# A two-block transformer layer on one core: the router and the expert rows taken from the weighted residual, with 1/rms applied at the exit, the shift added on GpSimd, and the biases split beside the output product

## The reference

```python
def rmsnorm(x, w):
    xf = x.astype(jnp.float32)
    var = jnp.mean(xf * xf, axis=-1, keepdims=True)
    return (xf * lax.rsqrt(var + EPS) * w.astype(jnp.float32)).astype(x.dtype)

def modulate(h, shift, scale):
    return h * (1.0 + scale) + shift

h = h + g1 * (mix_x.astype(h.dtype) @ w_out[l])
h = h + g2 * moe(modulate(rmsnorm(h, norm_mlp_w[l]), sh2, sc2), w_router[l], b_router[l], ...)

# in moe: top 4 of 32 experts, tokens sorted by expert into blocks of 128
logits = (xt @ w_router + b_router).astype(jnp.float32)
top_vals, top_idx = lax.top_k(logits, TOP_K)
weights = jax.nn.softmax(top_vals, axis=-1)
...
dest = start_pad[sorted_e] + (jnp.arange(n_assign) - start_unpad[sorted_e])
...
gu = xblk @ w_gu[e] + b_gu[e]
gate, up = jnp.split(gu, 2, axis=-1)
act = (up + 1.0) * gate * jax.nn.sigmoid(SWIGLU_ALPHA * gate)     # both clipped before
return act @ w_down[e] + b_down[e]
```

## Time and profile before

| quantity | value |
|---|---|
| median of 3 runs | 3365.12 us (3364.69 to 3377.49) |
| profiled execution | 3372.43 us, span 3370.6 us |
| TensorE busy | 3107.6 us, 92% of the span |
| VectorE, ScalarE, GpSimd busy | 65%, 50%, 6% |
| conversion of a unit, ScalarE L456 (ring) | 795 times, 1054 ns |
| conversion of a unit, VectorE L464 (ring) | 795 times, 1217 ns |

### The profile page before, as it was taken

One profiled execution on the slowest core, in us unless ns is written; L12 is line 12 of the kernel. 1 busy time (PEld: TensorE's weight loads), 2 busy tenths in 40 slices (PEclk: granted clock), 3 DMA queues, 4 the chain that ended last, 5 costly groups with the idle time before them and its releaser, 6 DMA issues.

```text
span 3370.6 us, 37642 instructions
## 1 busy us (share of the span) xinstructions
PE 3107.6 (92%) x14074; PEld 2450.5 (73%) x14074; DVE 2177.8 (65%) x2497; ACT 1677.6 (50%) x1935; POOL 188.6 (6%) x179
## 2 busy tenths in 40 slices
PE   6989857999999999999978978999998998999998
PEld 2865556777777777777766756888887766788887
DVE  4555436999999999999976444443456557544345
ACT  2332334878877877777764212332234246432234
POOL 1054200000000000000002000000000000000000
PEclk9998967999999999999987978999999999999999
DMA  6246527999999999999955202323232210223220
GB/s 207 68 135 219 192 94 274 373 371 374 372 377 367 372 375 370 374 373 373 363 206 195 94 25 88 90 91 103 91 107 75 81 45 1 69 88 106 88 69 26
DMA packets 229490, 654.15 MB, mean 194 GB/s; under 512 B 21592, under 2 KB 40294, under 8 KB 228438
## 3 DMA queue, kind: packets, MB, share of 16 engines
q1 hardware_dynamic: 207408, 575.61, 47.7%
q0 software_dynamic: 10992, 45.73, 3.6%
q10 hardware_dynamic: 10902, 30.35, 2.4%
HBM read 614.39 MB, written 37.22 MB: 193 GB/s over the span
## 4 chain that ended last, share of the span: by engine, by line
PE 81%; DVE 12%; ACT 4%; issue 2%; DMA 1%; POOL 0%; DVEq 0%; ACTq 0%; SPq 0%; POOLq 0%
PE ps L272 78%; PE ps L284 3%; DVE arena L203 2%; ACT arena L237 2%; DVE arena L192 2%; ACT wunits L456 2%; DVE arena L199 2%; DVE ring_r L464 1%; DVE arena L211 1%; DVE H L192 1%; DMA arena<-in_ctx 1%; DVE arena L197 0%; DVE arena L215 0%; DVE arena_r L203 0%; DVE arena_r L464 0%
## 5 line engine op out<-in xcount | busy, mean ns | idle before, releaser
L464 DVE TENSOR_TENSOR ring_r<-ring,wunits 128x1024 fp32r<-128x1024 f32 x795 | 943.4, 1217 | 674.2 <-ACT wunits L456 658.3
L456 ACT ACTIVATE wunits<-ring 128x1024 fp32r<-128x1024 f32 x795 | 830.6, 1054 | 814.6 <-PE ps L272 793.5
L272 PE MATMUL ps<-arena_r,wunits 128*128 128x512 f32 (+1 forms) x3552 | 1112.3, 395 | 19.5 <-DVE arena_r L192 13.9
L272 PE MATMUL ps<-wunits,arena_r 128*128 128x512 f32 x3520 | 991.7, 399 | 3.2 <-DVE arena_r L192 3.2
L272 PEld LDWEIGHTS ps<-arena_r,wunits 128*128 128x128 f32 x3552 | 672.4, 190 | 168.9 <-issue 23.9
L272 PEld LDWEIGHTS ps<-wunits,arena_r 128*128 128x128 f32 x3520 | 658.7, 189 | 148.6 <-DVE arena_r L192 5.0
L272 PE MATMUL ps<-arena_r,ring_r 128*128 128x512 f32 (+1 forms) x1776 | 695.3, 391 | 0.0
L272 PE MATMUL ps<-ring_r,arena_r 128*128 128x512 f32 x1280 | 410.3, 391 | 0.0
L272 PEld LDWEIGHTS ps<-arena_r,ring_r 128*128 128x128 f32 x1776 | 337.8, 190 | 70.3
L272 PE MATMUL ps<-arena 128*128 128x128 f32 (+11 forms) x1368 | 236.6, 354 | 87.3 <-DVE arena L215 19.8
L464 DVE TENSOR_TENSOR arena_r<-arena,wunits 128x1024 fp32r<-128x1024 f32 x240 | 283.6, 1220 | 17.7 <-ACT wunits L456 11.4
(11 more groups left out here) (147 smaller groups left out, 1874.0 us busy)
## 6 DMA issues: line engine op xcount, KB each, us to landing
ring<-in_w_gu SPq DMA_DIRECT2D x382, 512.0 KB, 6.9
ring<-in_w_down SPq DMA_DIRECT2D x170, 512.0 KB, 5.5
arena<-in_w_gu SPq DMA_DIRECT2D x146, 512.0 KB, 6.8
arena<-in_w_down SPq DMA_DIRECT2D x94, 512.0 KB, 5.7
ring<-in_w_ada SPq DMA_DIRECT2D x48, 512.0 KB, 4.6
ring<-in_ffn_w_gate SPq DMA_DIRECT2D x44, 512.0 KB, 3.5
ring<-in_ffn_w_up SPq DMA_DIRECT2D x44, 512.0 KB, 3.6
ring<-in_ffn_w_down SPq DMA_DIRECT2D x40, 512.0 KB, 3.6
```

Of the source, the lines that this page charges most:

```text
L272: ins = self.e.matmul(o, l_, r_, start=start, stop=stop, skip_group_check=True)
L456: q.inc(q.e.activation(h, raw, ACT.Copy), (st.tag, "hi", i))
L464: q.inc(q.e.tensor_tensor(lo, raw, h.bitcast(F32), ALU.subtract), (st.tag, "lo", i))
```

## The change

The norm of the second half is not applied before the router any more. `HM` is now the residual times the gain, made tile by tile by ScalarE right behind the residual (`tile_act`), and TensorE adds a tile's share to the logits beside its squares (`tile_pe`). 1/rms multiplies the logits on VectorE and the token rows on ScalarE, when they leave PSUM. What the shift adds is worked out once: `shift_pe` turns its columns into a row by products with the identity, multiplies them with the router weights, and spreads both over the partitions with a product of ones. GpSimd adds the row to the token rows and stores them (`rows_pool`). The router, bias and table loads stand at the head of the stage, `pair` stays on in it, so that the shift and the biases advance beside the tiles. The routing has its prefix counts from two products and five additions, compares eight assignments in one operation, and leaves the expert weights to the end. The eight `MORE` slots are filled once the first gather has landed.

```diff
     def fetch(s, st, i):
...
-            if w.before[0] == "all":
+            if w.before[0] == "gathered":
+                barrier_of(s, "moe")
+                s.wait_ge(s_g[0], 16)
+            elif w.before[0] == "all":
...
-    MORE = [[s_more[i], lo, 0, ("all", "moe")] for i, lo in enumerate(
+    MORE = [[s_more[i], lo, 0, ("gathered",)] for i, lo in enumerate(
...
+    def tile_act(q, k):
+
+        q.wait_ge(*dve("resid", "mlp", k))
         if k >= q.squares:
-            q.wait_ge(*pe("ssq", tag, k - q.squares))
-        q.act(sqt(q, k), hk(k), ACT.Square, ("sq", tag, k))
-        yield
-        yield
+            q.wait_ge(*pe("ssq", "mlp", k - q.squares))
+        q.act(sqt(q, k), hk(k), ACT.Square, ("sq", "mlp", k))
+        q.act(HM[:, k, :], hk(k), ACT.Copy, ("hm", k), scale=gm2[:, k:k + 1])
+        yield
...
+    def tile_pe(p, k):
...
         for m in range(4):
             p.mm(PB[b][:, 2 * m:2 * m + 2], sqt(p, k)[:, m * 128:(m + 1) * 128], ones[:, 0:2], k == 0 and m == 0, k == 7,
...
+        p.wait_ge(*act("hm", k))
+        for t in range(4):
+            p.mm(PB[bl][:, t * 32:(t + 1) * 32], HM[:, k, t * 128:(t + 1) * 128], wr[:, k, :], k == 0 and t == 0, k == 7,
+                 "logits" if k == 7 and t == 3 else None)
+        yield
...
+    def shift_pe(p):
...
+        for k in range(8):
+            p.mm(PB[bs[k // 4]][0:1, (k % 4) * 128:(k % 4 + 1) * 128], M(3, k), ident, k % 4 == 0, k % 4 == 3,
+                 ("shift", k // 4) if k % 4 == 3 else None)
+        for k in range(8):
+            p.mm(PB[bs[2]][0:1, 0:32], M(3, k), wr[:, k, :], k == 0, False)
+        p.mm(PB[bs[2]][0:1, 0:32], ones[0:1, 0:1], br, False, True, ("shift", 2))
+        yield
+        yield
+        p.wait_ge(*dve("shift rows"))
+        for c in range(3):
+            b = p.bank(("shifts", c))
+            p.claim(("shifts", c))
+            x = srow[c] if c < 2 else brow
+            p.mm(PB[b][:, 0:x.shape[1]], ones[0:1, :], x, True, True, ("shifts", c))
...
     def out_act(q):
         q.limit = None
-        for i in range(U_IN, U_IN + NUNIT):
-            conv_hi(q, W, i)
-        q.slow.append(biases_act(q))
-        split_act(q, "mix", mixp, lambda k: MX[:, k, :])
-        q.wait_ge(*dve("parts", "mix", 7))
         load(q, "router", wr, I["w_router"][0].rearrange("(j p) n -> p j n", p=128))
         load(q, "router", br, I["b_router"])
+        biases_load(q)
         tab(q, "tri", 19456)
...
+        for i in range(U_IN, U_IN + NUNIT):
+            conv_hi(q, W, i)
+        q.slow += [shift_act(q), biases_act(q)]
+        split_act(q, "mix", mixp, lambda k: MX[:, k, :])
+        dense(q, conv_hi, W, [512, 512], 8, lambda c, m: q.jobs.append(tile_act(q, c * 4 + m)))
...
     def router_act(q):
-        roots_act(q, "mlp")
-        for k in range(8):
-            q.wait_ge(*dve("hm", k))
-            q.act(HM[:, k, :], HM[:, k, :], ACT.Identity, "hm", bias=M(3, k))
...
-                q.copy(xs[t % 2][:, h * 512:(h + 1) * 512], bank_of(("hmt", t, h))[:, :])
+                q.act(xs[t % 2][:, h * 512:(h + 1) * 512], bank_of(("hmt", t, h))[:, :], ACT.Copy, ("row", t, h),
+                      scale=rt[:, 2 * t:2 * t + 1])
                 q.free(("hmt", t, h))
-            q.own()
-            q.e.dma_start(hm_d[t * 128:(t + 1) * 128, :], xs[t % 2]).then_inc(s_hm[t % 2], 16)
...
+    def rows_pool(g):
         for t in range(4):
             for h in range(2):
+                x = xs[t % 2][:, h * 512:(h + 1) * 512]
+                g.wait_ge(*act("row", t, h))
+                g.tt(x, x, SROW[:, h * 512:(h + 1) * 512], ALU.add)
+            g.own()
+            g.e.dma_start(hm_d[t * 128:(t + 1) * 128, :], xs[t % 2]).then_inc(s_hm[t % 2], 16)
...
     def route_dve(v):
...
+        v.tt(LG, bank_of("logits")[:, 0:128].rearrange("p (t e) -> p t e", e=32),
+             rt.rearrange("p (t x) -> p t x", x=2)[:, :, 0:1].to_broadcast([128, 4, 32]), ALU.mult)
+        v.tt(LG, LG, BROW.unsqueeze(1).to_broadcast([128, 4, 32]), ALU.add)
...
+        for h in range(2):
+            is_ = slice(8 * h, 8 * h + 8)
+            v.tt(LH[:, is_, :], iota.unsqueeze(1).to_broadcast([128, 8, 128]),
+                 OF4[:, is_].unsqueeze(2).to_broadcast([128, 8, 128]), ALU.is_equal)
+            v.tt(RP[:, is_, :], iota[:, 0:48].unsqueeze(1).to_broadcast([128, 8, 48]),
+                 BK4[:, is_].unsqueeze(2).to_broadcast([128, 8, 48]), ALU.is_equal)
+            for t in (2 * h, 2 * h + 1):
+                v.ts(RH[:, 4 * t:4 * t + 4, :], RP[:, 4 * t:4 * t + 4, :], tokc[:, t:t + 1], None, ALU.mult, None,
+                     ("slots", t))
...
-        for i in range(16):
-            if i >= 2:
-                v.wait_ge(*pe("slots", i - 2))
-            v.ts(LH[i % 2], iota, OF4[:, i:i + 1], None, ALU.is_equal, None)
-            v.ts(RH[i % 2], iota[:, 0:NBLK], BK4[:, i:i + 1], tokc[:, i // 4:i // 4 + 1], ALU.is_equal, ALU.mult,
-                 ("slots", i))
...
+        v.wait_ge(*act("weights"))
+        v.reduce(SS, W4, ALU.add)
+        v.recip(SS, SS)
+        v.tt(W4, W4, SS.unsqueeze(2).to_broadcast([128, 4, 4]), ALU.mult)
...
     def moe_pool(g):
+        g.wait_ge(*dve("idx"))
+        g.wait_ge(*pe("hmt", 3, 1))
...
         gla_pe(p)
+        out_pe(p)
         p.pair = False
-        out_pe(p)
...
-        all_wait(p, "moe")
+        p.note(("all", "moe"))
```

More of the change, by code:

```diff
@@ new lines, in tile_act @@
+    def tile_act(q, k):
+        q.wait_ge(*dve("resid", "mlp", k))
+        if k >= q.squares:
+            q.wait_ge(*pe("ssq", "mlp", k - q.squares))
[3 more added lines that the diff above has]
+    def tile_pe(p, k):
+        if k == 0:
+            p.inuse.append(p.bank("ssq"))
+            p.inuse.append(p.bank("logits"))
+            yield
+        b, bl = p.banks["ssq"], p.banks["logits"]
+        p.wait_ge(*act("sq", "mlp", k))
+        if k == 0:
+            p.claim("ssq")
+            p.claim("logits")
+        for m in range(4):
+            p.mm(PB[b][:, 2 * m:2 * m + 2], sqt(p, k)[:, m * 128:(m + 1) * 128], ones[:, 0:2], k == 0 and m == 0, k == 7,
+                 ("ssq", "mlp", k) if m == 3 else None)
+        p.wait_ge(*act("hm", k))
[3 more added lines that the diff above has]
+        yield
@@ new lines, in tile_dve @@
+    def tile_dve(v, k):
+        yield
+    def shift_pe(p):
+        bs = [p.bank(("shift", c)) for c in range(3)]
+        p.wait_ge(*loaded("router"))
+        p.wait_ge(*dve("gm2"))
+        for c in range(3):
+            p.claim(("shift", c))
+        for k in range(8):
[4 more added lines that the diff above has]
+        p.mm(PB[bs[2]][0:1, 0:32], ones[0:1, 0:1], br, False, True, ("shift", 2))
@@ L1708, in roots_act, with shift_act @@
-    def roots_act(q, tag):
-        q.finish_jobs()
-        q.wait_ge(*dve("var", tag))
-        q.act(rt, rt, ACT.Sqrt, ("rt", tag))
-    def roots_dve(v, tag):
-        v.finish_jobs()
-        v.wait_ge(*pe("ssq", tag, 7))
-        v.ts(rt, bank_of(("ssq", tag))[:, 0:8], 1.0 / 1024, EPS, ALU.mult, ALU.add, ("var", tag))
-        v.free(("ssq", tag))
-        v.wait_ge(*act("rt", tag))
-        v.recip(rt, rt)
-        for m in range(4):
-            v.ts(dg[:, m, :], ident, rt[:, 2 * m:2 * m + 1], None, ALU.mult, None, ("dg", tag, m))
-        v.wait_ge(*pe("rms", tag))
+    def shift_act(q):
+        yield
+        yield
+        yield
+        for c in range(2):
+            q.wait_ge(*pe("shifts", c))
+            q.copy(SROW[:, c * 512:(c + 1) * 512], bank_of(("shifts", c))[:, :], ("shifts", c))
+            q.free(("shifts", c))
+        yield
@@ new lines, in shift_dve @@
+    def shift_dve(v):
+        yield
+        for c in range(2):
+            v.wait_ge(*pe("shift", c))
+            v.copy(srow[c], bank_of(("shift", c))[0:1, :])
+            v.free(("shift", c))
+        v.wait_ge(*pe("shift", 2))
+        v.copy(brow, bank_of(("shift", 2))[0:1, 0:32], "shift rows")
+        v.free(("shift", 2))
+        yield
+        yield
+        v.wait_ge(*pe("shifts", 2))
+        v.copy(BROW, bank_of(("shifts", 2))[:, 0:32])
+        v.free(("shifts", 2))
+        yield
@@ L1948, in route_dve @@
         v.reduce(SEL, OH.rearrange("p (t k e) -> p t e k", k=4, e=32), ALU.add, "sel")
+        v.fill(PF[:, 0, :], 0.0)
         v.wait_ge(*pe("ranks"))
-        v.copy(RKf, bank_of("ranks")[:, 0:128])
-        v.copy(CNT, bank_of("ranks")[:, 128:160])
+        sums = bank_of("ranks")[:, 128:256].rearrange("p (t e) -> p t e", e=32)
+        for t in range(4):
+            v.tt(PF[:, t + 1, :] if t < 3 else CNT, PF[:, t, :], sums[:, t, :], ALU.add)
+        v.tt(RKf, bank_of("ranks")[:, 0:128], a(o + 2700, 128), ALU.add)
         v.free("ranks")
@@ L1973, in route_dve @@
         v.stt(DF, BK4, 128.0, OF4, ALU.mult, ALU.add)
-        v.copy(DEST, DF)
+        for h in range(2):
+            is_ = slice(8 * h, 8 * h + 8)
[6 more added lines that the diff above has]
+                     ("slots", t))
+        v.wait_ge(*pe("slots"))
```

(12 more changed lines are left out.)

154 lines of the change are left out of this document (56 added, 98 removed).

## The result

| | before | after |
|---|---|---|
| first runs: median (lowest to highest) | 3365.12 us (3360.95 to 3377.49, 5 runs) | 3347.63 us (3344.90 to 3348.56, 5 runs) |
| ratio, 95% interval | | 0.9935 [0.9912, 0.9959] |
| timed again, on one chip | 3364.46 us (13 runs) | 3340.46 us (3333.22 to 3350.54, 6 runs), ratio 0.9932 [0.9912, 0.9953] |
| profiled execution | 3372.43 us, span 3370.6, clock 0.945 | 3345.97 us, span 3344.1, clock 0.948 |
| barrier to the gathered block's first transposes | 375.19 to 530.69: 155.5 | 372.77 to 500.31: 127.5 |

The account below looks back on a forecast made before the run. Experts bound by TensorE, so an earlier first gather counts fully: +6.5 and +8.7, tail -10.9, -14.8, -15.1, gather -4.6 give 30.2 us less, from 3365.1 to 3335 us. Range 3320 to 3350.

Parts of the forecast that it names:

- one to one: Experts: bound by TensorE, so time won ahead of them should reach the kernel's end in full.
- Steps 1 and 2: Up to the output product's end: loads ahead of ScalarE's conversions, +6.5 us; more TensorE work inside the product, +8.7 us.
- Step 3: Behind the product: TensorE waits 10.9 us for ScalarE's bias copies and VectorE's subtractions before the first late square.
- Step 4: Tail behind the product: four tiles of 16 short passes at the lower clock after idle time, 14.6 us.
- Rival (a): Front better: tail keeps 2.4 GHz (7.6 us, not 14.6) or gather takes 3 us; together 3326 us; chance 0.12.
- Steps 5 and 6: Routing: VectorE begins once logits are ready, -14.8 us; wider operations sum to 21.5 us, 24 with GpSimd's share, from 39.1.
- Step 7: Routing: GpSimd's shift additions hold VectorE 2.5 us (0 to 9.9 possible); row stores end 3 us before indices, costing nothing.
- rival (b): GpSimd becomes the path: the lock's 7.4 us, or stores later by 10; 3342 us; chance 0.12.
- Step 8: First gather: 5.0 us instead of 9.59, as eight weight transfers now wait for it; landed at 500.3.
- (c): Experts bound by the weights' stream, so only its 20 us earlier start counts; 3345 us; chance 0.07.
- (d): Slower: pieces between the product's units let the clock fall to 1.2 GHz inside it; 3376 us; chance 0.07.
- (e): The change doesn't shorten: biases would still stand in the path; excluded by the order, no chance given.

Follow-up runs that it names:

- late_4: The change with four idle GpSimd additions ahead of the first gather; median 3348.71 us (8 runs).
- loads_on_pool: The change with the 13 loads issued by GpSimd behind the barrier instead of by ScalarE; median 3329.54 us.
- early_and_pool: biases_early with the 13 loads issued by GpSimd behind the barrier; median 3321.2 us, ratio to before 0.9874.
- biases_early: The change with bias parts drawn forward, the first behind the split, the others behind the product's second and third unit; median 3329.16 us, ratio to before 0.9902.
- gate_undone: The change with the eight held-back weight transfers waiting for routing and stores, as before, not the first gather; median 3335.41 us.

## Why the prediction came out so

- **What bounds it, and "one to one"**: right. Experts of 1173.98 and 1174.00 us, and late_4 (4.1 of 4.7 us arrive).
- **Steps 1 and 2** (+6.5, +8.7): right, +6.3 and +8.9; loads_on_pool and early_and_pool each take 6 to 7 us back.
- **Step 3** (10.9): right in mechanism and size (11.5); biases_early removes 9.6 of it. The steps count three tiles in the product and four in the tail; the fourth tile, 2.0 us, stands in this wait, so that it cost nothing and TensorE was idle for 9.5 us, not 10.9.
- **Step 4** (14.6): the number was right (13.9), its reason was not, so it is luck in part. "TensorE will have been idle for 11 us, so I take that level again" fails: in biases_early and early_and_pool the tail takes 12.7 and 13.0 us without that idle time, which cost about 1 us of it. Rival (a)'s tail of 7.6 us was not to be had that way.
- **Steps 5 and 6**: VectorE began at once, and alone the routing is as costed: 27.6 - 5.7 = 21.9 against 21.5.
- **Step 7**, the mis-sized term: 2.5 us of contention, measured 5.6 to 5.7, inside the 0 to 9.9 named. "Most of its operations here are short and read one tile" misled: five short ones waited, by 0.9 to 1.6 us each (1.87 for one that takes 0.3 alone), for what was left of an addition, however short they are themselves. The half of rival (b) that is this lock came in part. With the Trainium skill's rule (SBUF — State Buffer, "SBUF: two separate sides"), an exclusive lock for a whole instruction, the rows agree: four of the five that waited have two inputs in SBUF, and a reduction beside an addition did not wait (1036 ns against 1020). The fifth, at 478.74, has one input of 128 elements (1.16 us against 0.24 alone), which fits the same section's second case, an operation in a two-port mode; no row shows the mode itself. The stores' cover was wide: the last was issued at 483.65, 12 us ahead of the gather, and they took 2.9 us in the median, not 4.4.
- **Step 8**: the size was right (4.5 against 5.0), the cause only half: gate_undone shows that the reordered VectorE work frees the gather, and the new gate adds nothing.
- **The sum**: 28.0 of 30.2 in the stage. The first median, 3347.6, is 12.6 us above the 3335 and outside the forecast's 3329 to 3341, because the step from the stage to the median was too simple: I took the 7.3 us of the profiled execution over the median for noise around one value, where there are two groups, some 13 us apart. That 3347.6 is inside the range of 3320 to 3350 is luck: its upper part stood there for rivals (b) and (c), and what filled it is a stage that no rival names. The change's lower group has its median at 3334.6 us; that it is so near 3335 is in part luck too, since the lower group of before has 3362.7, not the 3365.1 that the sum starts from, and the change takes 28.1 from it.
- **Rivals**: (a) falls, the tail took 13.9 us and the gather 4.5; (c) falls, no transfer is waited for; (d) falls, the clock is 1.00 in the product from 400 us on, as in the kernel before; (e) falls as stated, though the biases do stand in the path, in a new place.

## What to carry to other kernels

Cost a change in the stage where it acts, from one event to the next in two traces, and then look for stages far behind it that changed although the change doesn't touch them: here one draws between 338 and 353 us, and three runs say little about the median. Work that is moved "beside" a product needs its own chain laid out step by step (copy, subtraction, copy), and is free only if its last link ends before the product does. When several things are changed at a queue (a gate, an order, a wait), undo them one at a time: the one with the name was not the one that paid.

## Not expected of the hardware

- The same program's attention stage ran at a mean clock of 0.87 or 0.96 and took 352.9 or 339.6 us, with the same dates until then but for 0.7 us; the stage from the 528-pass to the first 1408-pass group too took 344.8 to 353.7 us, with the same instructions.
- TensorE's clock fell from 1.00 to 0.50 within its own work, 1 to 2 us into 64 short passes that followed a product with 0.2 us of idle time (biases_early).
- GpSimd's 1.27 us additions lengthened single VectorE operations on 16 or 32 elements a partition from 0.2 us to 1.17 and 1.29, and in late_4 one with one input of 16 elements to 1.09.
